# First weight chunk in halves, a per-tile final norm, another place for the short quarter, and gate rows split during the attention

## The reference, cut to what matters

```python
def rmsnorm(x, w):
    xf = x.astype(jnp.float32)
    y = xf * lax.rsqrt(jnp.mean(xf * xf, axis=-1, keepdims=True) + RMS_EPS)
    return (y * w.astype(jnp.float32)).astype(x.dtype)
...
        h = modulate(rmsnorm(x, norm_mix_w[i]), sh_m, sc_m)
        hc = modulate(rmsnorm(ctx, norm_mix_w[i]), shc_m, scc_m)
        if i % 2 == 0:
            y, y_c = ab_mixer(h, hc, ab_w_in[j], ab_w_out[j], ab_sgu_norm_w[j], ab_sgu_w[j], ab_sgu_b[j],
                              ab_rel_bias[j], not last)
...
        x = x + g_m * y
        x = x + g_f * swiglu(modulate(rmsnorm(x, norm_ffn_w[i]), sh_f, sc_f), ffn_w_gate[i], ffn_w_up[i], ffn_w_down[i])
...
    return rmsnorm(x, final_norm_w)
```

## Time and profile before

| | |
|---|---|
| median of 3 runs | 3325.37 us (3324.85 to 3326.69) |
| the profiled execution's own time | 3324.33 us |
| its span in the trace | 3322.5 us |
| TensorE (PE) busy | 3182.1 us, 96% |
| DVE busy | 1694.6 us, 51% |
| ACT busy | 1201.7 us, 36% |
| DMA engines, mean | 104 GB/s over the span |

### The profile page before, as it was taken

One profiled execution on the slowest core, in us unless ns is written; L12 is line 12 of the kernel. 1 busy time (PEld: TensorE's weight loads), 2 busy tenths in 40 slices (PEclk: granted clock), 3 DMA queues, 4 the chain that ended last, 5 costly groups with the idle time before them and its releaser, 6 DMA issues. The chain is left out here.

```text
span 3322.5 us, 41325 instructions
## 1 busy us (share of the span) xinstructions
PE 3182.1 (96%) x17152; PEld 2631.6 (79%) x17152; DVE 1694.6 (51%) x2441; ACT 1201.7 (36%) x1830; POOL 1.2 (0%) x6
## 2 busy tenths in 40 slices
PE   8889999999999999999999998899999999999998
PEld 6767888888776788888887866799998777578886
DVE  5745546554343665555433346587773545443233
ACT  4415443222325445322234226453342433342222
POOL 0000000000000000000000000000000000000000
PEclk9999999999999999999999999999999999999999
DMA  4212326774232032577522400333335442043331
GB/s 140 75 58 89 115 65 163 182 188 127 76 119 75 26 107 84 142 183 184 152 76 83 99 23 1 111 87 109 97 105 188 137 129 78 12 116 90 101 114 70
DMA packets 427434, 346.87 MB, mean 104 GB/s; under 512 B 24040, under 2 KB 362536, under 8 KB 426992
## 3 DMA queue, kind: packets, MB, share of 16 engines
q1 hardware_dynamic: 411152, 334.96, 33.8%
q10 hardware_dynamic: 16096, 9.26, 1.1%
HBM read 333.39 MB, written 10.80 MB: 104 GB/s over the span
## 5 line engine op out<-in xcount | busy, mean ns | idle before, releaser
L379 DVE TENSOR_TENSOR w_lo<-raw,w_hi 128x1024 fp32r<-128x1024 f32 (+1 forms) x454 | 523.1, 1194 | 742.6 <-ACT w_hi L366 742.0
L366 ACT CAST w_hi<-raw 128x1024 fp32r<-128x1024 f32 (+1 forms) x454 | 443.4, 1026 | 992.8 <-PE ps L422 727.4
L420 PE MATMUL ps<-slots,w_hi 128*128 128x512 f32 (+1 forms) x1680 | 660.6, 393 | 28.9 <-DVE w_lo L379 16.2
L422 PE MATMUL ps<-slots,w_lo 128*128 128x512 f32 (+1 forms) x1680 | 643.0, 383 | 0.0
L421 PE MATMUL ps<-slots,w_hi 128*128 128x512 f32 (+1 forms) x1680 | 642.2, 382 | 0.0
L420 PEld LDWEIGHTS ps<-slots,w_hi 128*128 128x128 f32 x1680 | 317.2, 189 | 102.2 <-issue 23.8
L421 PEld LDWEIGHTS ps<-slots,w_hi 128*128 128x128 f32 x1680 | 317.2, 189 | 64.6 <-issue 6.3
L422 PEld LDWEIGHTS ps<-slots,w_lo 128*128 128x128 f32 x1680 | 316.9, 189 | 62.2
L420 PE MATMUL ps<-w_hi,hT_hi 128*128 128x512 f32 x536 | 214.7, 400 | 8.6 <-DVE hT_lo L1797 5.5
L420 PE MATMUL ps<-hT_hi,w_hi 128*128 128x384 f32 (+3 forms) x592 | 207.1, 350 | 4.1 <-ACT arena L1121 1.8
L421 PE MATMUL ps<-w_lo,hT_hi 128*128 128x512 f32 x536 | 209.6, 391 | 0.0
(11 more groups left out here) (432 smaller groups left out, 4934.0 us busy)
## 6 DMA issues: line engine op xcount, KB each, us to landing
scratch_sb<-in_ada_w SPq DMA_DIRECT2D x96, 512.0 KB, 6.4
raw<-in_ffn_w_in SPq DMA_DIRECT2D x88, 512.0 KB, 7.3
raw<-in_ffn_w_down SPq DMA_DIRECT2D x30, 1024.0 KB, 5.1
raw<-in_ffn_w_gate SPq DMA_DIRECT2D x44, 512.0 KB, 3.9
raw<-in_ffn_w_up SPq DMA_DIRECT2D x44, 512.0 KB, 5.2
raw<-in_ffn_w_out SPq DMA_DIRECT2D x20, 1024.0 KB, 5.1
raw<-in_ev_w_in SPq DMA_DIRECT2D x16, 1024.0 KB, 5.4
raw<-in_xa_w_kv SPq DMA_DIRECT2D x16, 1024.0 KB, 5.3
```

Source lines behind the costliest of these rows:

```text
L366: act.copy(self.split_chunk(c)[0][:, half], self.raw_chunk(c)[:, half]).then_inc(self.split_hi, 1)
L379: ins = dve.tensor_tensor(lo[:, half], self.raw_chunk(c)[:, half], hi[:, half].bitcast(F32), ALU.subtract)
L420: pe.matmul(out, w[0], x[0], start=first, stop=False, skip_group_check=more)
L422: return pe.matmul(out, w[1], x[0], start=False, stop=last, skip_group_check=more)
```

## The change

It has four parts. The first weight chunk is loaded and split in two halves by rows of the sum, and TensorE waits for the second half only when it comes to it; ACT's first table load gets an instruction of its own ahead of the data, and the squares of `setup` move behind all splits. The norm at the end is done per token tile inside `out_project`, by a class `Final`, whose weights are loaded with the gate tables. In `ffn_out0`, `glu_out0` and its side, and `glu_out1` the short quarter is the fifth instead of the sixth (`SHORT_INSIDE`). In `ab_mixer` rows 0 to 3 of `y` are split during the first units of the context attention into buffers of their own, and `out_both` begins with them without a join; the low part of rows 4 to 7 goes to another place, and the side rows' first low part waits until the matmuls on the early rows are over.

```diff
+SHORT_INSIDE = (0, 4, 8, 12, 20, 16)
...
-        by_quarters(I["ffn_w_out"][l], KF)
+        by_quarters(I["ffn_w_out"][l], KF, ks=SHORT_INSIDE if l == 0 else None)
...
-            by_quarters(I["ffn_w_down_2"][l], KF)
+            by_quarters(I["ffn_w_down_2"][l], KF, ks=SHORT_INSIDE)
...
-            if g == of[i][0]:
+            halved = first + i in k.halved and g == of[i][0]
+            if g == of[i][0] and not halved:
                 k.wait_split(pe, first + i)
...
             for kk in range(KD):
+                if halved and kk == KD // 2:
+                    k.wait_split(pe, first + i)
                 k.wait_h(pe, kk, "x" if a < SEQ else "side")
...
+        if final:
+            act.activation(k.stat[:, 63:64], k.ones[:, 0:1], ACT.Sqrt)
         for t in range(TX):
...
+            if final and t:
+                inverted(dve, t - 1)
+                dve.wait_ge(*s_rstd(nth[t - 1]))
+                final.vector(dve, t - 1, rstd[:, t - 1:t], slice(0, D))
+        if final:
+            inverted(dve, TX - 1)
+            dve.wait_ge(*s_rstd(nth[TX - 1]))
+            for cols in (left, right):
+                final.vector(dve, TX - 1, rstd[:, TX - 1:TX], cols)
...
         def side_low(q):
             dve.wait_ge(*s_side_hi(q + 1))
+            if ahead and q == 0:
+                dve.wait_ge(*s_used(2))
...
-                dve.tensor_tensor(k.lo[:, slots(q), 0:SEQ], main_rows(q),
-                                  k.hi[:, slots(q), 0:SEQ].bitcast(F32), ALU.subtract).then_inc(*s_y_lo.up(1))
+                dve.tensor_tensor(main_lo(q), main_rows(q), main_hi(q).bitcast(F32), ALU.subtract).then_inc(*s_y_lo.up(1))
...
+            if ahead and 2 <= u < 2 + KQ:
+                dve.wait_ge(*s_ahead_hi(u - 1))
+                dve.tensor_tensor(ahead[2][:, u - 2], ahead[0][:, u - 2], ahead[1][:, u - 2].bitcast(F32),
+                                  ALU.subtract).then_inc(*s_ahead_lo.up(1))
...
+            if ahead and 1 <= u < 1 + KQ:
+                act.copy(ahead[1][:, u - 1], ahead[0][:, u - 1]).then_inc(*s_ahead_hi.up(1))
...
+        sp.dma_start(raw[:, low], src[:, low]).then_inc(k.landed[RING], 16)
         for i in range(4):
             sp.dma_start(k.XT[:, 2 * i:2 * i + 2], x[:, 2 * i:2 * i + 2]).then_inc(*s_x[i].up(16))
             if i == 0:
-                k.stream(sp, -1)
+                sp.dma_start(raw[:, high], src[:, high]).then_inc(k.landed[k.slot_of[0]], 16)
...
+    def sync(self, sp):
+        k, parts = self.k, self.parts()
+        for i, (t, cols) in enumerate(parts):
+            sp.wait_ge(*self.s_done(i + 1))
+            sp.dma_start(k.out[0, t * P:(t + 1) * P, cols], self.o[:, t, cols]).then_inc(k.out_stored, 16)
+        sp.wait_ge(k.out_stored, 16 * len(parts))
```

More of the change, by code:

```diff
@@ L1266, in out_project @@
 def out_project(k, name, first, y, kt, gate=None, loads=(), early=(), flow=False, tiles=tuple(range(TX)),
-                banks=tuple(range(8)), ahead=False, others=None, norm=True, turned=None):
+                banks=tuple(range(8)), ahead=False, others=None, norm=True, turned=None, starts=None, final=None):
     nk = -(-kt // KQ)
@@ L1289, in out_project @@
     order = sides + list(range(TX)) if norm else []
-    nth = {t: i + 1 for i, t in enumerate(order)}
+    nth = {t: i + 1 for i, t in enumerate(order if norm else range(TX))}
     left, right = slice(0, BANK), slice(BANK, D)
@@ L1620, in side, with out_both @@
         return self.sides[:, q % 2, 0:r.stop - r.start]
[L1623 removed]
+def out_both(k, name, first, side_first, y, kt, gate, loads, l, which, early=(), values=None, fetched=None, ahead=None):
     nk = -(-kt // KQ)
     n = 2 * nk
[L1626 removed]
+    size = lambda q: min(KQ, kt - (fetched.starts[q] if fetched else q * KQ))
     slots = lambda q: slice(KQ * (q % 2), KQ * (q % 2) + size(q))
@@ L2712, in setup @@
     x = I["xT"].rearrange("(k p) n -> p k n", p=P)
+    (src,), (low, high) = k.chunks[0][2], k.halves(0)
+    raw, (w_hi, w_lo) = k.raw_chunk(0), k.split_chunk(0)
+    k.halved.add(0)
     @block.sync
@@ L2727, in _ @@
     def _(act):
+        act.wait_ge(*s_filled(1))
+        act.mul(k.stat[:, 63:64], k.ones[:, 0:1], k.ones[:, 0:1])
+        act.wait_ge(k.landed[RING], 16)
+        act.copy(w_hi[:, low], raw[:, low]).then_inc(k.split_hi, 1)
         act.wait_ge(*s_cols(16))
@@ L2733, in _ @@
             if i == 0:
[L2734 to L2738, removed]
+                k.wait_landed(act, 0)
+                act.copy(w_hi[:, high], raw[:, high]).then_inc(k.split_hi, 1)
+                k.next_hi = 1
+        for m in range(KD):
             columns.square(act, m)
@@ L2748, in _ @@
         dve.wait_ge(*s_filled(1))
+        dve.wait_ge(k.split_hi, 1)
+        dve.tensor_tensor(w_lo[:, low], raw[:, low], w_hi[:, low].bitcast(F32), ALU.subtract)
         dve.wait_ge(*s_cols(16))
@@ L2754, in _ @@
             if i == 0:
[L2755 to L2760, removed]
+                dve.wait_ge(k.split_hi, 2)
+                dve.tensor_tensor(w_lo[:, high], raw[:, high], w_hi[:, high].bitcast(F32), ALU.subtract).then_inc(k.split_lo, 1)
+                k.next_lo = 1
+        for m in range(1, KD):
             columns.add(dve, m)
@@ new lines, in swiglu, with __init__, parts, vector @@
+    final = Final(k, A)
+    out_project(k, f"gluo{l}", W[f"glu_out{l}"], rows, KF, gate, loads + [final.load], norm=False, early=[(ahead, s_y_lo(KQ))],
+                flow=True, banks=(0, 1, 2, 6, 7, 3, 4, 5), starts=SHORT_INSIDE, final=final)
+class Final:
+    def __init__(self, k, A):
+        self.k, self.w, self.o = k, A(D), A(TX, D)
+        self.s_done, = stage_sems(k, "final", "dve:done")
+        fw = k.ins["final_norm_w_2"]
+        self.load = (self.w, bass.AP(fw.tensor, fw.offset, [[0, P], [1, D]]))
+    def parts(self):
+        whole = [(t, slice(0, D)) for t in range(TX - 1)]
+        return whole + [(TX - 1, slice(0, BANK)), (TX - 1, slice(BANK, D))]
+    def vector(self, dve, t, rstd, cols):
+        dve.scalar_tensor_tensor(self.o[:, t, cols], self.k.X[:, t, cols], rstd, self.w[:, cols], ALU.mult,
+                                 ALU.mult).then_inc(*self.s_done.up(1))
+    def sync(self, sp):
[4 more added lines that the diff above has]
+        sp.wait_ge(k.out_stored, 16 * len(parts))
```

96 lines of the change are left out of this document (43 added, 53 removed).

## The result

| | median us | single runs |
|---|---|---|
| before | 3325.37 | 3324.85 to 3326.69 (5) |
| after | 3307.15 | 3300.03 to 3308.46 (5) |
| profiled execution of after | 3308.46 | span 3306.6 |

The ratio is 0.9942, with a 95% interval of 0.9929 to 0.9954: 18.2 us less, where 20 had been forecast. The profiled execution is the longest of the five. On another chip the two stood at 3302.96 and 3324.95, ratio 0.9933 (0.9919 to 0.9946), 22.0 us less. The span of the profiled execution is 15.9 us shorter. The places are taken in the order of the prediction.

The account below looks back on a forecast made before the run. TensorE was busy 96% of the span, leaving its pauses, low clock and the two ends to gain. Terms 2.9 + 6.6 + 2.9 + 1.5 + 6.6 = 20.5 us off 3322.5 gave 3302.0, plus 1.8 and 1.0: 3305 us, range 3299 to 3312.

Parts of the forecast that it names:

- case A: Whole kernel: all terms come as forecast, time near 3305 us; chance 0.60.
- Start: Kernel start: half-chunk loading lets PE begin near 9.2 us; gain 1.7 or 3.4 us, taken as 2.9.
- ffn_out0: Short quarter fifth in ffn_out0: DVE keeps up, waits and slow matmuls go; 6.6 us less, bounds 2.85 and 6.7.
- abo: At abo: 8.1 us gained by early rows, less a 3.6 us wait and 1.6 us of slow matmuls; net 2.9.
- glu_out0: Around glu_out0: two waits go, the transpose's grows, a 0.8 us side-part wait arises; 1.5 us less, bounds -1 and 3.
- The end: Behind the last matmul: norm per tile and half stores shorten the chain; 6.6 us less.
- the other order: Last projection with its short quarter last: DVE would end about 5 us late.
- (B): Rival at abo and start: early rows come free, start gives all of its 3.4; 3302 to 3298 us; chance 0.13.
- The earlier trace: Used for the clock at abo: it stayed at 1.00 where PE was busy only 3.51 of 6.50 us.
- (C): Rival in three projections: short quarter only moves waits, ffn_out0 gives 2 or less, glu_out0 loses 1; 3312 us; chance 0.19.
- (D): Rival: no measurable change, only the end's 6.6 holds, stretched attention eats abo's gain; 3319 to 3322 us; chance 0.06.
- (E): Rival at abo: slower, DVE's block makes four side chunks late by up to 8.2 us each; 3338 us; chance 0.02.

Follow-up runs that it names:

- e2: Kernel before with only the short quarter fifth in ffn_out0: 3317.58 us, ratio 0.9971 against before.
- e8: Kernel before with only the short quarter fifth in glu_out0, side rows too: 3327.38 us, ratio 1.0006 against before.
- e7: Changed kernel with the short quarter last again in glu_out1, the norm per token tile kept: 3307.07 us, 4.1 more than the changed kernel.
- e1: Kernel before with only the end changed (norm per token tile, last projection's short quarter fifth): 3318.75 us, ratio 0.9975 against before.
- e3: Kernel before with only abo changed (first quarter's rows split in the attention): 3325.16 us, ratio 0.9995 against before.
- e10: Changed kernel with abo's third-chunk low part first, plus glu_out0's short quarter last again, side rows too: 3301.01 us, 1.8 more than without the latter.
- e12: Changed kernel with abo's third-chunk low part first, plus another TensorE order in glu_out1's last quarter: 3297.65 us, 1.5 less than without the latter.

## Why the prediction was right

The forecast was 3305 us (3299 to 3312), and 3307.15 and, elsewhere, 3302.96 came out: case A. Point by point:

- **Start**, 2.9: the pair of traces gives 2.90. Over all profiles PE's second group began at 20.55 to 22.43 us with the old start (five) and at 17.02 to 18.62 with the new one (nine), means 21.6 and 17.9, so 3.6 is the better size. One detail was off: PE began at 10.06 and not near 9.2, since XT's first pair landed at 8.4 instead of 7.7. It cost little, since PE was then held for the second pair until 12.79, as forecast (12.8), and behind that by no arrival.
- **`ffn_out0`**, 6.6: 6.9 in after and in e2. All three waits and the eight slow matmuls went.
- **`abo`**, 2.9: the mechanism held (a wait of 3.75 us for the 3.6 forecast, slow matmuls behind it), and the size of the clock's part varied. In the profiled pair the whole term is 1.2, under half of the forecast. The product took 64.3 to 65.5 us in the five traces with the old code and 62.63, 63.76, 61.22 and 63.71 in the four with the new one: 2.1 us on average, with 5, 11, 0 and 11 steps of 0.43 us where 8 had been charged. The first matmul behind the wait is one more slow one.
- **`glu_out0`**, 1.5: the offset gives 1.4, in after and in e8. The waits give 1.1, as the one at the transpose grew by 1.0, not 0.7, and the new one is 0.97, not 0.8. In the time it can't be seen.
- **The end**, 6.6: 7.3. Of the 0.7, 0.4 is the half store's landing (2.4 for 2.8), and 0.3 the small steps (the last store is issued 2.95 us behind X). The cost of the other order, 5 us in the prediction, was 2.7 in e7.
- What the sum left out is the clock between the places. I gave it a part in (B), in `ffn_out0`, at the start and in `abo` only, but slow stretches moved in work that the change doesn't touch, and took back some 3.8 us in the profiled pair. The earlier trace rows was used as a pause that leaves the clock up; it did so in before, but in e1, e2, e3 and e10 the clock fell in the same stretch.
- Part of the closeness is luck: the end gave 0.7 more than its term and `abo` 0.8 (on average) less, and which run is the median of five that spread over 8 us decides the rest.
- (B) fell by the wait; (C) by e2, though the wait that it named in the side part came (0.97 us); (D) by e1 and e2; (E) by the trace: behind 2102.76 PE waits for no further weight chunk in `abo`.

## What to carry to other kernels

When work is done ahead so that one wait goes, look at what is queued behind the instruction that now waits for its buffer: here one condition that moved a weight chunk's low part ahead of such an instruction gave back some 6 us, nearly as much as the largest part of the change. A short piece of the sum should not stand last where the vector engine needs longer per bank than the short piece's matmuls take: it cost 6.9 us at `ffn_out0`, and 2.7 at the very end. In `glu_out0`, where the short chunks cover less than the next chunk's split, moving it gave nothing that could be measured. Judge edits of 1 to 2 us by the waits in the trace, since slow stretches of the clock elsewhere are worth as much.

## What the runs showed of the hardware

- **The clock behind a pause is not fixed for a kernel.** Behind the same wait of 3.75 us four executions ran 5, 11, 0 and 11 slow steps; behind the pause near 1070 us the granted clock was 0.50 in one execution of a kernel and 1.00 in another. In the stretch of the earlier trace rows it fell in four kernels' traces (a mean of 0.83 over 10 us in e1, e2, e3 and e10), and stayed at 1.00 in before. It fell every time in five traces behind the wait of 2.85 us at `ffn_out0`, and in five behind that of 5.50 at `abo`. The Trainium skill (TensorE: Matmul & The Clock Gate, Part 1) tells of the same at a kernel's start, 6, 11 or 14 slow matmuls in runs of one kernel; the traces agree, with 7 slow steps at the old start in e1 and 12 in e8, and show it in mid-kernel as well. Summed as above, the slow clock is 25.8 us in e2 and 39.1 in e12. Which execution gets which was not found, and no kernel was made that shifts a pause alone.
- **Landings at the start vary by 2 us.** With one and the same start the first weight chunk (1 MB) was there at 9.27, 9.89, 10.00, 11.44 and 11.52 us; PE began 3.5 us behind it each time. With halves the first half was there at 5.13 to 6.28 us (nine executions), and PE's start varied by 1.1 us (9.53 to 10.66), where with the whole chunk it was 2.2 (12.77 to 15.01).
